# Router products in pairs on two column groups, and router weights loaded through GpSimd's queue

## The chip, the core and the metric

One core of a Trainium2 chip runs the whole program. A core has TensorE (matrix products, PE in the profile, its weight loads as PEld), VectorE (DVE), ScalarE (ACT), GpSimd (POOL) and SyncE (SP), which share an on-chip memory of 128 partitions; products go to PSUM, here eight banks `pb[0]` to `pb[7]` of 128 x 512 float32. Transfers are issued by SP, ACT and POOL, each into a queue of its own (q1, q10 and q0 in the profile), and run on the core's 16 DMA engines. The metric is device time in microseconds (us), lower is better. Before the change the median of three runs is 1541.58 us (1539.56 to 1543.03).

## The reference, cut to what matters

One decoder layer for 256 prompt tokens and 8 sample tokens, D = 2048, all in float32:

```
h  = RMSNorm(x);  q, k, v, u = h @ w_in          # 4 MB of w_in per 512 columns
x += [dilated attention | causal pooling] @ w_out
x += cross_attention(RMSNorm(x), 256 memory rows) @ w_co
h  = RMSNorm(x)
lg = h @ w_rg + b_rg                              # 4 expert groups: top 1
le = h @ w_re + b_re                              # 32 experts in 4 groups of 8: top 2 in the group
x += sum over the chosen experts of gate * SwiGLU_expert(h)
```

The step also returns the key and value caches of 8 sample rows shifted by one position: some 100 MB that are copied from DRAM to DRAM. The change concerns `lg` and `le`, which the kernel computes as one product with 36 columns.

## The kernel before, in words

Each engine runs its own written-out list of instructions, and semaphores order them; no planner is involved. All 264 tokens stand transposed in `xT`: 16 tiles of 128 channels x 264 tokens.

**Start.** SP loads the memory rows, `w_ck` in four parts, the tokens and `w_cv` (L437 to L445). ACT issues small loads first (L1279 to L1287), the last of them the router weights `w_rg` and `w_re` into `wr` (128 partitions x 16 x 36, a run of 4 or of 32 floats at a time: 2048 runs each) and the bias `b_re`. Only then does ACT square the memory rows and the tokens for the norms (L1288 to L1298). DVE makes diagonal matrices of the roots (L1635), and PE turns them into a row of scales (L705), for which it waits. Before that, PE computes the memory keys (L689) and two bias tables (L697, L699); after it the memory values and the turned tokens (L713, L718).

**Weights in a ring of two.** The 4 MB pieces (`w_ck`, `w_cv`, seven of `w_in`, `pool_w`, four of `w_out`, `w_cq`, `w_co`) go to two places in turn: `big(i)` on SP first waits until PE has used piece i - 2. PE works on them in order: L713 and L663 for `w_cv`, L663 and L669 for `w_in`, L745 for the rest of it, L909 for `w_out`, L927 for `w_cq`, L1041 for `w_co`.

**Cache copies.** ACT issues the 64 copies of the caches, 1.5 MB each, between its other work (`cache_part`, L1261), so their times follow PE's.

**GpSimd** only issues loads: constants at the start, the bias table (L596, then L599, four loads), and from L602 on the cache rows for the sample tokens, for which it waits until the sample queries are stored.

**Cross-attention's output and the router.** `for o in range(KT)` (L1037) computes the 16 channel tiles of the output: four products (L1041), DVE adds the tile to `xT` (L1872), ACT squares it, DVE adds the squares up (L1788). `route(k)` (L1014) multiplies tile k by `wr`, two tiles behind, and adds in bank 4. At the end ACT copies the 36 x 264 sums to `LT` (L1514), PE turns them to tokens (L1059), and DVE chooses experts from L1905 on. At every fourth tile the sample rows are turned (L1034).

**Experts.** SP streams the weights of 32 experts, 12.6 MB each, into the same ring and a third place; `gate_up(0, 0, 1)` (L521) waits for `w_co` to be used, the quarters of expert 1 (L495) for the first products of expert 0 (L1157).

`router_landed` is waited for once, at L1779, by DVE, which then scales `wr` by the norm's gains (L1780); PE waits for that at L1011.

Of the kernel before, what the change touches and what calls it, by code (L numbers as in the profile page):

```python
# [15 lines left out]
P = 128  # L16
D = 2048
KT = D // P
# [3 lines left out]
TOK = SEQ + NB  # L22
# [12 lines left out]
NG, EG = 4, 8  # L35
NE = NG * EG
# [111 lines left out]
def hybrid_decoder_layer(nc, a):  # L148
    with ExitStack() as ctx:
# [3 lines left out]
        def sb(name, shape, dt=F32):  # L153
            return ctx.enter_context(nc.sbuf_tensor(name, shape, dt))
# [5 lines left out]
        xT = sb("xT", [P, KT, TOK])  # L160
# [3 lines left out]
        ident = sb("ident", [P, P])  # L164
# [16 lines left out]
        slots = sb("slots", [P, 2, 3])  # L181
        gates = sb("gates", [P, 2, 3])
        ov_i = sb("ov_i", [1, OVB + 1], I32)
        top_i = sb("top_i", [P, 3, 8], U32)
# [97 lines left out]
        xn = Z[:, 3 * D:6 * D].rearrange("p (t n) -> p t n", t=3)  # L282
        LT = wr[:].rearrange("p k n -> p (k n)")[0:36, 0:TOK]
        xfree = xT[:].rearrange("p k t -> p (k t)")
# [273 lines left out]
        def _(pool):  # L558
# [39 lines left out]
            for r in range(0, P, REPS):  # L598
                pool.dma_start(bias[r:r + REPS],  # L599
                               bass.AP(tensor=bias_dram.tensor, offset=P - 1 - r, ap=[[384 - 1, REPS], [384 * REPS, H], [1, SEQ]]))\  # L600
                    .then_inc(bias_landed, 16)
            pool.wait_ge(pads_ready, 1)  # L602
            pool.wait_ge(mem_stored, 2 * 16)
# [32 lines left out]
        def _(pe):  # L636
# [377 lines left out]
            def route(k):  # L1014
                pe.wait_ge(co_added, k + 1)
                last = mm(pb[4][0:36, 0:TOK], wr[:, k, :], xT[:, k, :], start=(k == 0), stop=(k == KT - 1))  # L1016
                if k == KT - 1:
                    last.then_inc(logits_filled, 1)
# [18 lines left out]
            for o in range(KT):  # L1037
                if o >= 4:
                    pe.wait_ge(co_added, o - 3)
                for h in range(XH):  # L1040
                    last = mm(pb[o % 4][:, 0:TOK], wo[:, h, P * o:P * o + P], oT[:, h, :], start=(h == 0), stop=(h == XH - 1))  # L1041
                last.then_inc(co_filled, 1)
                if o >= 2:
                    route(o - 2)
                if o >= 5 and o % 4 == 1:
                    sample_rows_back((o - 5) // 4)
# [10 lines left out]
            for t in range(3):  # L1057
                n = P if t < 2 else NB
                last = turn(bk[0:n, 36 * t:36 * t + 36], LT[:, P * t:P * t + n], ident[0:36, 0:36])  # L1059
            last.then_inc(v_filled, 1)  # L1060
# [173 lines left out]
        def _(act):  # L1234
# [49 lines left out]
            act.dma_start(grow[4 * KT + UT:NGAIN], a["cq_norm_g"]).then_inc(first_landed, 16)  # L1284
            for w, lo, n in (("w_rg", 0, NG), ("w_re", NG, NE)):
                act.dma_start(wr[:, :, lo:lo + n], a[w][0].rearrange("(k p) n -> p k n", p=P)).then_inc(router_landed, 16)  # L1286
            act.dma_start(b36[:, NG:36], a["b_re"].to_broadcast([P, NE])).then_inc(router_landed, 16)  # L1287
            act.wait_ge(zeros_ready, 2)  # L1288
# [224 lines left out]
            act.wait_ge(logits_filled, 1)  # L1513
            copy(LT, pb[4][0:36, 0:TOK]).then_inc(logits_copied, 1)  # L1514
            roots(st[:, 3:6], st[:, 6:9])
# [41 lines left out]
        def _(dve):  # L1557
# [14 lines left out]
            def link(ins):  # L1572
                nonlocal nseq
                nseq += 1
                ins.then_inc(dve_seq, 1)
                dve.wait_ge(dve_seq, nseq)
# [201 lines left out]

            dve.wait_ge(router_landed, 3 * 16)  # L1779
            TT(wr[:], wr[:], gT[:, 3 * KT:4 * KT].unsqueeze(2).to_broadcast([P, KT, 36]), ALU.mult).then_inc(wr_scaled, 1)  # L1780

# [341 lines left out]
```

## Time and profile before

| | |
|---|---|
| median of 3 runs | 1541.58 us |
| profiled execution | 1531.4 us, its span 1529.6 us |
| PE busy | 1269.7 us (83%) |
| DVE, ACT, POOL busy | 531.1, 167.7, 62.6 us |
| DMA | 609.34 MB, mean 398 GB/s |
| mean granted TensorE clock | 0.888 of 2.4 GHz |

The page counts an engine as busy while it computes; an instruction that issues a transfer stands under the engine's queue (ACTq, SPq). DMA share is the mean busy share of the 16 DMA engines; it can go a little over 1, since packets overlap. The chain is the sequence of work that ended last, followed back from the end; its shares sum to the span.

### The profile page before, as it was taken

The page shows a single profiled execution, that of the slowest core. Times are in us where ns is not written, and L with a number is a line of the kernel's source. Part 1 is how long each engine was busy: PE and PEld are TensorE (multiplying, and loading weights), DVE is VectorE, ACT ScalarE, POOL GpSimd, SP SyncE. Part 2 cuts the span into 40 slices and gives each one's busy share as a digit, 9 for nine tenths or more (in the row PEclk, how much of TensorE's full clock was granted, in tenths as well). Part 3 has the DMA queues.
Part 4 walks back from the last instruction along what each step waited for, and adds up shares of the span by engine and source line. Part 5 has one row for each costly group of instructions (what it writes and reads, how often), then busy time and mean ns, then how long its engine had stood idle before and what let it go on. Part 6 is the DMA issues. An engine that isn't in the chain of part 4 may idle for free.

```text
span 1529.6 us, 23145 instructions
## 1 busy us (share of the span) xinstructions
PE 1269.7 (83%) x9913; PEld 626.5 (41%) x9913; DVE 531.1 (35%) x1102; ACT 167.7 (11%) x395; POOL 62.6 (4%) x115
## 2 busy tenths in 40 slices
PE   7799999998999999887867777777787677778777
PEld 4354458774887866322222222222222222222222
DVE  1040064750112334534334333433433433333344
ACT  0410012321111244000000000000000000000000
POOL 2000012212010000000000000000000000000000
PEclk9899999999999999988888788878887878778789
DMA  9999999989999999999999999999999999999997
GB/s 346 316 332 399 327 329 382 382 311 375 379 399 400 359 389 355 403 429 426 429 433 426 430 432 431 425 429 434 425 429 434 425 429 434 425 429 429 431 428 309
DMA packets 101909, 609.34 MB, mean 398 GB/s; under 512 B 11390, under 2 KB 13065, under 8 KB 78929
## 3 DMA queue, kind: packets, MB, share of 16 engines
q1 hardware_dynamic: 55027, 477.14, 75.0%
q10 hardware_dynamic: 38822, 101.11, 18.1%
q0 software_dynamic: 8016, 30.46, 5.7%
q8 instruction: 33, 0.54, 0.1%
q14 instruction: 11, 0.09, 0.0%
HBM read 603.09 MB, written 106.75 MB: 464 GB/s over the span
## 4 chain that ended last, share of the span: by engine, by line
DMA 53%; PE 40%; ACTq 3%; DVE 1%; issue 1%; ACT 1%; SPq 1%; DVEq 0%
DMA ring<-in_w_e_up_dram 44%; PE pb L1157 12%; PE pb L663 6%; PE pb L909 6%; DMA ring<-in_w_out_dram 5%; DMA ring<-in_w_in_dram 4%; PE pb L745 4%; ACTq L1286 2%; PE pb L1041 2%; PE pb L927 2%; PE pb L713 1%; SPq L486 1%; PE pb L669 1%; PE pb L1016 1%; PE pb L1191 1%
## 5 line engine op out<-in xcount | busy, mean ns | idle before, releaser
L1157 PE MATMUL pb<-ring,xT 128*32 128x256 f32 x4096 | 285.7, 441 | 123.4 <-DMA ring<-in_w_e_up_dram 118.7
L1157 PEld LDWEIGHTS pb<-ring,xT 128*32 128x32 f32 x4096 | 143.5, 126 | 285.7 <-DMA ring<-in_w_e_up_dram 156.5
L2040 DVE TENSOR_TENSOR Z<-pb,Z 128x512 f32<-128x512 f32 x248 | 152.7, 679 | 253.1 <-PE pb L1110 253.1
L1093 PE MATMUL pb<-Z,xT 128*32 128x512 f32 (+1 forms) x768 | 137.1, 808 | 94.8 <-DVE Z L2040 91.7
L1110 PE MATMUL pb<-xT 32*128 32x512 f32 x744 | 168.7, 751 | 0.0
L1191 PE MATMUL pb<-ring,xT 128*32 128x512 f32 x960 | 136.9, 722 | 0.0
L663 PE MATMUL pb<-ring,hreg 128*128 128x512 f32 (+1 forms) x320 | 125.7, 552 | 2.6 <-DMA ring<-in_w_in_dram 2.6
L1093 PEld LDWEIGHTS pb<-Z,xT 128*32 128x32 f32 (+1 forms) x768 | 16.6, 117 | 185.7 <-DVE Z L2040 118.9
L663 PEld LDWEIGHTS pb<-ring,hreg 128*128 128x128 f32 x320 | 60.1, 190 | 65.1 <-issue 59.2
L909 PE MATMUL pb<-hreg,ring 128*128 128x264 f32 x320 | 78.3, 402 | 5.8 <-DMA ring<-in_w_out_dram 5.8
L745 PE MATMUL pb<-hreg,ring 128*128 128x264 f32 x320 | 75.3, 395 | 1.0 <-DMA ring<-in_w_in_dram 1.0
L2037 DVE TENSOR_TENSOR Z<-pb,Z 128x512 f32<-128x512 f32 x31 | 21.4, 692 | 144.7 <-remote 84.1
L909 PEld LDWEIGHTS pb<-hreg,ring 128*128 128x128 f32 x320 | 62.3, 199 | 17.0 <-DMA ring<-in_w_out_dram 6.5
L745 PEld LDWEIGHTS pb<-hreg,ring 128*128 128x128 f32 x320 | 61.2, 194 | 13.4 <-DMA ring<-in_w_in_dram 1.4
L1191 PEld LDWEIGHTS pb<-ring,xT 128*32 128x32 f32 x960 | 32.1, 130 | 78.2 <-issue 77.5
L2064 DVE TENSOR_SCALAR xT<-xT 128x128 f32<-128x128 f32 x32 | 7.3, 227 | 148.4 <-ACT xT L1533 148.4
L1110 PEld LDWEIGHTS pb<-xT 32*128 32x128 f32 x744 | 30.5, 154 | 67.0 <-issue 67.0
L1533 ACT ACTIVATE xT<-pb 128x128 f32<-128x128 f32 x32 | 8.9, 278 | 421.8 <-PE pb L1157 421.8
L1535 ACT COPY xT<-pb 128x264 f32<-128x264 f32 x32 | 12.2, 381 | 313.9 <-PE pb L1102 313.9
L1791 DVE TENSOR_TENSOR xT<-pb,xT 128x264 f32<-128x264 f32 x16 | 6.9, 433 | 111.6 <-PE pb L909 111.6
L909 PE MATMUL pb<-Z,ring 128*128 128x264 f32 x192 | 45.4, 386 | 0.0
L1657 DVE COPY Z<-pb 128x512 f32<-128x512 f32 (+1 forms) x5 | 3.2, 638 | 104.5 <-PE pb L663 104.5
(333 smaller groups left out, 1117.2 us busy)
## 6 DMA issues: line engine op xcount, KB each, us to landing
ring<-in_w_e_gate_dram SPq DMA_DIRECT2D x61, 2048.0 KB, 18.6
ring<-in_w_e_up_dram SPq DMA_DIRECT2D x61, 2048.0 KB, 23.1
ring<-in_w_e_down_dram SPq DMA_DIRECT2D x30, 4096.0 KB, 18.9
out_win_k_sample_dram<-in_cache_win_k_dram ACTq DMA_DIRECT2D x24, 1536.0 KB, 15.4
out_win_v_sample_dram<-in_cache_win_v_dram ACTq DMA_DIRECT2D x24, 1536.0 KB, 14.0
ring<-in_w_in_dram SPq DMA_DIRECT2D x7, 4096.0 KB, 32.9
ring<-in_w_out_dram SPq DMA_DIRECT2D x4, 4096.0 KB, 32.7
out_win_k_sample_dram<-in_cache_win_k_dram ACTq DMA_DIRECT2D x8, 1488.0 KB, 15.0
```

The costliest lines, as they stand in the source:

```text
L663: last = mm(bk[:, 0:n], xt[:, k, tile * P:tile * P + P], w[:, k, 0:n], start=(k == 0), stop=(k == KT - 1))
L745: last = mm(bk[:, 0:TOK], w[:, k, :], hT[:, k, :], start=(k == 0), stop=(k == KT - 1))
L909: last = mm(bk[:, 0:TOK], w[:, k, :], mix(k), start=(i == 0), stop=(i == KT - 1))
L927: last = mm(bk[:, 0:TOK], wk(CQ)[:, k, XD * h:XD * h + XD], xT[:, k, :], start=(k == 0), stop=(k == KT - 1))
L1041: last = mm(pb[o % 4][:, 0:TOK], wo[:, h, P * o:P * o + P], oT[:, h, :], start=(h == 0), stop=(h == XH - 1))
L1093: last = mm(pb[0][32 * c:32 * c + 32, :], pick[0:n, t, :], xn[0:n, t, 512 * c:512 * c + 512], start=(t == 0), stop=(t == 2))
L1110: last = mm(out, GT[r, cols], yo[r, :], start=True, stop=True)
L1157: last = mm(pb[1][32 * c:32 * c + 32, 0:256], XT[:, k, :], w[:, :, k8, P * c:P * c + P], start=(k == 0), stop=(k == KT - 1))
L1191: last = mm(pb[3][32 * c:32 * c + 32, :], aT[:, 32 * f:32 * f + 32], w[f][:, 512 * c:512 * c + 512], start=(f == 0), stop=(f == 3))
L1286: act.dma_start(wr[:, :, lo:lo + n], a[w][0].rearrange("(k p) n -> p k n", p=P)).then_inc(router_landed, 16)
L2037: last = V.tensor_tensor(x3s, banks[0][:, :], x3s, ALU.add)
L2040: last = V.tensor_tensor(d, banks[c][:, :], d, ALU.add)
```

## The change

Two things are changed. The three loads of the router's weights and of `b_re` go from ACT's list, ahead of its squares, to GpSimd's list, behind the four loads of the bias table. And `route` is called in pairs after every odd tile: even tiles go to partitions 0 to 35 of bank 4, odd tiles to partitions 64 to 99 (another group of TensorE's columns), each half with its own start and stop; the two halves are copied by two ACT instructions, and the turn to tokens becomes a product with `both36`, two identities stacked at rows 0 and 64 with zeros between, so that it adds the halves. Of `LT` the rows 36 to 63 hold what is left of `wr`, and meet zeros.

```
+        both36 = sb("both36", [P, 36])
-        LT = wr[:].rearrange("p k n -> p (k n)")[0:36, 0:TOK]
+        LT = wr[:].rearrange("p k n -> p (k n)")[:, 0:TOK]
 GpSimd, behind the bias table's loads:
+            for w, lo, n in (("w_rg", 0, NG), ("w_re", NG, NE)):
+                pool.dma_start(wr[:, :, lo:lo + n], a[w][0].rearrange("(k p) n -> p k n", p=P)).then_inc(router_landed, 16)
+            pool.dma_start(b36[:, NG:36], a["b_re"].to_broadcast([P, NE])).then_inc(router_landed, 16)
             pool.wait_ge(pads_ready, 1)
 TensorE:
             def route(k):
                 pe.wait_ge(co_added, k + 1)
-                last = mm(pb[4][0:36, 0:TOK], wr[:, k, :], xT[:, k, :], start=(k == 0), stop=(k == KT - 1))
+                r = 64 * (k % 2)
+                last = mm(pb[4][r:r + 36, 0:TOK], wr[:, k, :], xT[:, k, :], start=(k < 2), stop=(k >= KT - 2))
...
-                if o >= 2:
+                if o >= 3 and o % 2:
+                    route(o - 3)
                     route(o - 2)
...
-                last = turn(bk[0:n, 36 * t:36 * t + 36], LT[:, P * t:P * t + n], ident[0:36, 0:36])
+                last = mm(bk[0:n, 36 * t:36 * t + 36], LT[0:100, P * t:P * t + n], both36[0:100, :], start=True, stop=True)
 ScalarE, start:
-            for w, lo, n in (("w_rg", 0, NG), ("w_re", NG, NE)):
-                act.dma_start(wr[:, :, lo:lo + n], a[w][0].rearrange("(k p) n -> p k n", p=P)).then_inc(router_landed, 16)
-            act.dma_start(b36[:, NG:36], a["b_re"].to_broadcast([P, NE])).then_inc(router_landed, 16)
 ScalarE, behind the loop:
-            copy(LT, pb[4][0:36, 0:TOK]).then_inc(logits_copied, 1)
+            copy(LT[0:36], pb[4][0:36, 0:TOK])
+            copy(LT[64:100], pb[4][64:100, 0:TOK]).then_inc(logits_copied, 1)
 VectorE, behind its wait for router_landed:
+            link(V.memset(both36[:], 0.0))
+            V.tensor_copy(both36[0:36], ident[0:36, 0:36])
+            V.tensor_copy(both36[64:100], ident[64:100, 64:100])
```

## Rows read from the trace of the kernel before

**Rows 1.** The page's chain that ended last, shares of the span by line.

```profile
DMA ring<-in_w_e_up_dram 44%; PE pb L1157 12%; PE pb L663 6%; PE pb L909 6%; DMA ring<-in_w_out_dram 5%; DMA ring<-in_w_in_dram 4%; PE pb L745 4%; ACTq L1286 2%; PE pb L1041 2%; PE pb L927 2%; PE pb L713 1%; SPq L486 1%; PE pb L669 1%; PE pb L1016 1%; PE pb L1191 1%
```

**Rows 2.** The chain in order of time, 0 to 60 us: start, us, what.

```profile
5.57 30.33 ACTq L1286
35.94 3.18 ACTq L1287
...
54.76 2.00 PE pb L713 x2
...
57.16 1.06 PE pb L713 x2
```

**Rows 3.** The timeline, 0 to 60 us: start, us, engine, line; brackets: idle before, releaser.

```profile
20.82 0.30 PEld L689 LDWEIGHTS pb<-ring 128*128 128x128 f32 x2 [1.30 <-DMA ring<-in_w_ck_dram]
...
42.36 0.80 PE L699 MATMUL pb<-qkm,psm 33*128 33x321 f32 x2
...
53.02 1.74 PE L705 MATMUL pb<-Z,ones 128*128 128x128 f32 x6 [9.86 <-DVE Z L1635]
```

**Rows 4.** Stretches at the start and of a w_in piece: last columns PEclk, DMA share, GB/s.

```profile
37.50:42.50 5.00, 5.00 (x13) 1.76 (x12) 0.00 (x0) 3.28 (x4) 0.00 (x0) 1.00 0.65 59
80.00:93.00 13.00, 13.00 (x36) 6.01 (x35) 11.55 (x28) 1.05 (x4) 0.00 (x0) 1.00 0.70 229
93.00:125.80 32.80, 31.99 (x197) 15.81 (x196) 3.69 (x4) 2.69 (x7) 0.00 (x0) 1.00 1.03 387
```

**Rows 5.** The one DMA issue of 92.5 to 93.2 us: size, us to landing.

```profile
ring<-in_w_in_dram SPq DMA_DIRECT2D x1, 4096.0 KB, 32.9
```

**Rows 6.** TensorE's timeline, 120 to 178 us, where it starts on the second and third piece.

```profile
125.48 14.00 PE L663 MATMUL pb<-ring,hreg 128*128 128x512 f32 x32 [0.81 <-DMA ring<-in_w_in_dram]
158.78 14.00 PE L663 MATMUL pb<-ring,hreg 128*128 128x512 f32 x32 [1.76 <-DMA ring<-in_w_in_dram]
```

**Rows 7.** DMA packets and queues of 5 to 42 us, then of 700 to 1400 us.

```profile
DMA packets 6342, 12.42 MB, mean 336 GB/s; under 512 B 5034, under 2 KB 5203, under 8 KB 5305
q10 hardware_dynamic: 4612, 0.37, 11.2%
DMA packets 17186, 300.72 MB, mean 430 GB/s; under 512 B 1904, under 2 KB 1904, under 8 KB 1904
```

**Rows 8.** POOL's timeline: the bias table's loads and the next one.

```profile
64.48 2.48 POOL L599 DMA_DIRECT2D ring<-bias_rows  x4 [9.41 <-DMA bias_rows<-qkm]
206.44 0.59 POOL L562 DMA_DIRECT2D ring<-in_cache_win_k_dram  x1 [139.49 <-DMA out_win_k_sample_dram<-Z]
```

**Rows 9.** The chain in order of time, the output loop and two comparisons: start, us, what.

```profile
292.58 0.80 PE pb L792 x8
...
561.39 0.57 PE pb L1016 x2
561.96 1.98 PE pb L1041 x8
...
570.12 1.78 PE pb L1041 x8
...
614.75 3.63 PE pb L1157 x64
```

**Rows 10.** DVE's timeline, 366 to 376 us.

```profile
370.61 0.74 DVE L1780 TENSOR_TENSOR wr<-wr,gT 128x576 f32<-128x576 f32 x1
```

**Rows 11.** The timeline behind the loop, 590 to 600 us.

```profile
596.91 0.63 PEld L1053 LDWEIGHTS pb<-ones,Z 128*128 128x128 f32 x6 [0.48 <-DVE Z L1788]
596.95 0.37 ACT L1514 COPY wr<-pb 36x264 f32<-36x264 f32 x1 [0.56 <-PE pb L1016]
597.57 0.34 PE L1059 MATMUL pb<-ident,wr 36*128 36x36 f32 x3
```

**Rows 12.** Stretches behind the output loop; columns as in rows 4.

```profile
588.00:598.00 10.00, 9.97 (x49) 6.33 (x48) 3.39 (x11) 3.24 (x8) 0.00 (x0) 1.00 0.88 299
612.00:616.00 4.00, 4.00 (x75) 2.27 (x67) 2.90 (x16) 0.00 (x0) 0.00 (x0) 1.00 0.65 219
```

## The prediction

> **What bounds the kernel now.** I read the page's chain first, then the chain and the timeline of its two places that the change touches, then the DMA's stretches between them. By line the chain is the stream of expert weights for nearly half of the span and products for most of the rest; a single entry is neither, ACT's queue at L1286 with 2% [rows 1]. In order of time that entry is one instruction: the issue of `w_re` holds ACT's list from 5.57 us for 30.33 us, and `b_re` for 3.18 us more [rows 2]. The squares behind it give the scales late: PE has ended its last bias table (L699) at 43.16 us and stands still for 9.86 us, until L705 at 53.02 us [rows 3]. So the start is bound by an issue, not by data.
>
> From 93 us on the DMA is full, share 1.03 [rows 4]: a 4 MB piece of `w_in` issued there needs 32.9 us to land [rows 5], and PE waits for the pieces, 0.81 and 1.76 us at the second and third [rows 6]. At the output loop the chain is PE's products alone [rows 9]; at its end and behind it the DMA has a little room, 0.88 for 10 us and 0.65 for 4 us [rows 12]. Behind it the experts' stream runs at 430 GB/s [rows 7] to the end; it can only be moved earlier as a whole.
>
> **The change part by part.** All against the profiled execution, 1531.4 us.
>
> *ACT without the issues.* 33.5 us of issues go [rows 2]. ACT then squares as soon as rows and tokens are there, and what is late next is PE itself, which cannot take the scales before it has ended L699. So not 33.5 us are won but PE's idle time, 9.86 us. Beside it goes the clock's price: after the pause L705 takes 1.74 us [rows 3] and the first pair of L713 2.00 us, where a later pair takes 1.06 [rows 2]. The engine had stood still, and half speed (1.2 of 2.4 GHz) doubles an instruction; L705 at half its time wins 0.87, L713 0.94, together 1.8 us. Third, the small packets of `w_rg` and `w_re` leave the first loads alone: the weight loads' 1.30 us of waiting for `w_ck` [rows 3] may shrink; the bounds are 0 and 1.3, I take 1.0. PE reaches the memory values 9.9 + 1.8 + 1.0 = 12.7 us earlier.
>
> *The same loads on GpSimd.* POOL has two waits that could be touched: the four loads of the bias table stand ahead, so they lose nothing; behind, POOL waits 139.49 us for the sample queries until 206.44 us [rows 8], or to 194 us when all is 12.7 us earlier. How long POOL needs to issue runs of 16 and 128 bytes, no row shows. Bounds: 0.62 us each, as L599's four in 2.48 us [rows 8], and ACT's 33.5 us in all [rows 2]. I take the first for the sum; either is hidden by that wait: from about 56 us (the bias loads' end, 67 us, less 11) the cover lasts 138 us. The data is wanted at 370 us, where DVE scales it [rows 10].
>
> *The DMA's share.* The packets do not go away. Between 5 and 42 us ACT's queue took 11.2% of 16 engines, 4.1 us of all of them; from the other side, 336 GB/s moved there against 430 GB/s later [rows 7] leaves 37 x (1 - 336/430) = 8.1 us. That work now lies behind 56 us, where room is scarce: 37.5 to 42.5 us had 0.35 x 5 = 1.8 us free and 80 to 93 us 0.30 x 13 = 3.9 us [rows 4], and both close, since ACT's copies stand behind its squares and now begin earlier. The cost on the path is what the second and third piece of `w_in` land later than 12.7 us ahead of now. In the full stretch SP's queue gets its part whatever the backlog of the copies, and a piece takes 32.9 us either way [rows 5]; a third queue slows it only while the small packets last. Bounds 0 and 8.1 us; I take 2, nearest to half of the 4.1, since some of it falls before the piece is issued. That the copies' own backlog costs nothing is assumed: it is the first rival. Start, net: 12.7 - 2 = 10.7 us.
>
> *The pairs.* A `route` costs the chain 0.57 us [rows 9] and a slower restart: the eight products of a tile take 1.98 us behind it, 1.78 us behind a turn [rows 9]. So 0.57 + 0.20 = 0.77 us each. Two halves of the array at work together are shown by L792: eight matmuls in two groups of 64 columns, 4 x 256 and 4 x 128 columns long, take 0.80 us [rows 9]; one after the other at L663's rate (14.00 us for 32 of 512 columns [rows 6], 0.85 ns a column) it would be 1.31. Four groups gain more, 64 of 256 columns in 3.63 us [rows 9] against 14.0. So I price a pair at 0.77 + 0.1 us, not at 1.54: seven pairs in the loop save 7 x 0.67 = 4.7 us. Bounds: 7 x 0.20 = 1.4 us if they do not overlap at all and only a restart is saved, 7 x 0.77 = 5.4 us if the second is free.
>
> What is late next is the DMA. The copies and loads of the loop are the same, in less time. The room was 0.12 x 10 + 0.35 x 4 = 2.6 us [rows 12]; beyond that the experts' stream begins behind the same work. The share is no hard wall (1.03 in [rows 4]), so I take 3.0 us, bounds 0 and 4.7.
>
> *The end of the router.* The second ACT copy costs at most another 0.37 us, and the product with `both36` has two passes where the turn had one: 0.34 us more at most [rows 11]. The copy is hidden: PE's next work, L1053, waits for DVE's squares and not for the products [rows 11], and the last pair ends before the three products of now did. Without that cover it is 0.37 us. I count 0. DVE's three new small instructions stand ahead of the scaling at 370 us; each is far smaller than its 0.74 us [rows 10], and the loop that wants it begins 190 us later [rows 9]: 0, and 2.2 us if that cover were gone.
>
> The Trainium skill, TensorEngine Tiling, Key Properties, says that a change of the tiling mode drains TensorE. The 0.20 us restart agrees; by that rule alone, without overlap, the loop would save the lower bound.
>
> Sum: 10.7 + 3.0 = 13.7 us, so 1517.7 us for a profiled execution. That one lay 10.2 us under the median of the runs; I carry the difference over: 1541.58 - 13.7 = 1528 us. With everything kept it is 9.9 + 1.8 + 1.3 + 4.7 = 17.7 us less, 1524; with 8.1 us given back and no gain in the loop 4.6 us less, 1537.
>
> **The rivals.**
>
> *The DMA takes most of it back.* If the stretch from 93 us on is bound by the sum of its packets and not by SP's part of them, the pieces land only as much earlier as DMA room is found: 1.8 + 3.9 us [rows 4] less the 2 to 4 us of small packets, so 2 to 4 us, and 1 to 2 us at the loop. That gives 4 to 6 us, 1536 us. For it: share 1.03 and two waits of PE for pieces. Against it: 80 to 93 us had room, and two of the copies go out before PE's products for the keys end. The Trainium skill has this as a rule in DMA: Bandwidth & Descriptors, Issuing engines are not separate DMA queues: loads from another engine share the same 16 engines, and only issue time is saved. The rows bear out both halves: issue time is what the chain shows.
>
> *The pairs do not overlap.* Then the loop saves 1.4 us or nothing, the start stays: some 11 us, 1531 us. Against it are L792 and L1157 in [rows 9].
>
> *GpSimd is held as ACT was, and longer: slower than before.* If the two loads of short runs hold POOL's list, the cache rows of the sample tokens come late, and through DVE's sample scores and PE's turns the whole kernel does. It decides from the point where POOL is not free by 194 us, that is when three issues from about 56 us take over 138 us, four times ACT's 33.5 [rows 2], with now two other queues beside them. At five times, 167 us, everything behind is 30 us late, less 13.7: 16 us slower, 1558 us. Against it: L599's 0.62 us an issue [rows 8].
>
> *It does not do what it says.* Some other condition holds the scales back, such as the tokens' landing; then the start gains under 3 us and the whole stays within the measurement's reach: 1540 us. Against it: nothing else stands ahead of ACT's squares but landings, and PE's keys and tables last to 43 us [rows 3].
>
> **How the numbers follow.** Forecast (1523 to 1533) 0.60; DMA takes it back 0.19; no overlap 0.08; does nothing 0.07; slower 0.06. The likeliest gives 1528 us. The range 1522 to 1537 holds the first three but for the upper part of the second, 0.8 in all. About 0.2%, 3 us, is what a measurement of this kernel can tell from no change: faster 0.60 + 0.08 + 0.18 = 0.86, the same 0.08, slower 0.06.
>
> **What would show it.** ACT's first square at about 8 us and not behind 39 us; L705 with under 1 us of idle time ahead of it, near 42 us, at the full granted clock; the third piece of `w_in` landing near 148 us, not 158.7 (if near 155, the first rival is right). Two `route` rows beside each other in 0.6 to 0.7 us, the loop 4.7 us shorter from L1041's first to its last product; the first quarter of expert 1 issued 15 us earlier if both parts carry, with no DMA room left before it. POOL's issues of `wr` over before 100 us. An idle POOL row of less than 50 us ahead of L562 would speak for the slower case. A `w_in` wait of PE over 5 us at L663 would prove my 2 us too small.

## The result, and the profile after

The changed kernel takes 1521.1 us in the median of four runs (1518.74 to 1529.45) against 1541.47 us of the kernel before (1539.56 to 1543.03): a ratio of 0.9887, with a 95% interval of 0.986 to 0.9915, that is 17.4 us less (13.1 to 21.6). The forecast was 13.7 us less, 1528, with a range from 1522 to 1537. The direction was right and the gain was 4 us larger. The median of 1521.1 lies 0.9 us below the range; by the ratio, on the earlier median of 1541.58, the time is 1524, inside it.

The profiled execution of after took 1520.75 us, close to its median; that of before, 1531.4, lay 10 us under its own. So the two traces differ by 10.7 us where the runs differ by 17.4 (by the ratio) to 20.4 (by the medians), and a trace can show where the gain arises but not all of its size. Starts on TensorE in the two traces, with the line of before / after:

| point | before | after | shift |
|---|---|---|---|
| scales, L705 / L709 | 53.02 | 43.60 | -9.4 |
| third piece of `w_in`, L663 / L667 | 158.78 | 145.82 | -13.0 |
| output loop, L1041 / L1046 | 555.81 | 544.95 | -10.9 |
| behind the loop, L1053 / L1059 | 596.91 | 580.74 | -16.2 |
| expert 0, L1157 / L1163 | 610.75 | 594.93 | -15.8 |
| expert 1, first half of its gate and up weights | 628.28 | 613.93 | -14.4 |
| expert 1, last quarter of them | 636.29 | 623.41 | -12.9 |

The page's chain by line, against [rows 1]: ACT's queue is gone, the streams stand as before.

```profile
DMA ring<-in_w_e_up_dram 45%; PE pb L1163 12%; PE pb L667 6%; PE pb L913 5%; DMA ring<-in_w_in_dram 4%; PE pb L749 4%; DMA ring<-in_w_out_dram 2%; PE pb L931 2%; PE pb L1046 2%; PE pb L693 2%; PE pb L717 1%; PE pb L867 1%; DMA qkm<-Z 1%; SPq L487 1%; PE pb L673 1%
```

ACT's timeline of after (start, us, engine, line; in brackets the idle time before it and its releaser), against [rows 2]: the first square starts at 7.29 us, the tokens' squares wait for the tokens' landing alone, and the first copy of the caches goes out at 33.12 us.

```profile
7.29 1.91 ACT L1273 ACTIVATE hreg<-Z 128x2048 f32<-128x2048 f32 x1
...
25.81 1.91 ACT L1273 ACTIVATE hreg<-Z 128x2048 f32<-128x2048 f32 x1 [9.89 <-DMA Z<-in_x_prompt_dram]
...
33.12 0.70 ACTq L1267 DMA_DIRECT2D out_win_k_sample_dram<-in_cache_win_k_dram  x1
```

TensorE's timeline of after, against [rows 3, 6]: no pause ahead of L709, its six products in 1.03 us and not 1.74, a first pair of L717 in 1.13 us (2.08 in before), and of the first three w_in pieces only the third is waited for.

```profile
42.86 0.80 PE L703 MATMUL pb<-qkm,psm 33*128 33x321 f32 x2
43.60 1.03 PE L709 MATMUL pb<-Z,ones 128*128 128x128 f32 x6
44.55 1.13 PE L717 MATMUL pb<-ring 128*128 128x512 f32 x2
...
145.82 14.00 PE L667 MATMUL pb<-ring,hreg 128*128 128x512 f32 x32 [0.98 <-DMA ring<-in_w_in_dram]
```

POOL's timeline of after, against [rows 8]: the three issues that held ACT for 33.9 us (0.41 for `w_rg`, and the 30.33 and 3.18 of [rows 2]) take 1.18, 1.16 and 0.56 us here, and the wait behind them is still 134.87 us long.

```profile
54.95 2.48 POOL L600 DMA_DIRECT2D ring<-bias_rows  x4 [10.36 <-DMA bias_rows<-qkm]
57.41 1.18 POOL L604 DMA_DIRECT2D wr<-in_w_rg_dram  x1
58.59 1.16 POOL L604 DMA_DIRECT2D wr<-in_w_re_dram  x1
59.73 0.56 POOL L605 DMA_DIRECT2D b<-in_b_re_dram  x1
195.16 0.55 POOL L563 DMA_DIRECT2D ring<-in_cache_win_k_dram  x1 [134.87 <-DMA out_win_k_sample_dram<-Z]
```

The DMA of after, packets of 5 to 42 us:

```profile
DMA packets 2651, 13.90 MB, mean 376 GB/s; under 512 B 775, under 2 KB 938, under 8 KB 1609
```

The same of 57 to 76 us, in which the three loads are issued and land (issue lines: size, us to landing):

```profile
DMA packets 2487, 6.74 MB, mean 355 GB/s; under 512 B 165, under 2 KB 213, under 8 KB 2485
...
wr<-in_w_re_dram POOLq DMA_DIRECT2D x1, 256.0 KB, 14.7
wr<-in_w_rg_dram POOLq DMA_DIRECT2D x1, 32.0 KB, 13.9
b<-in_b_re_dram POOLq DMA_DIRECT2D x1, 16.0 KB, 14.9
```

The reader is to see two things. Of the 5034 packets under 512 B of [rows 7], 4259 have left the first 42 us. And they have not come back: between 57 and 76 us there are 165 such packets in all, while 304 KB of router weights and bias land; up to 600 us they are 4457 against 8636 in before. ACT's queue moved them in runs of 16 and 128 bytes; through GpSimd's queue the records show no such runs.

The stretches of [rows 4] in after (last columns: granted TensorE clock, DMA share, GB/s): the two holes of before, 59 and 229 GB/s, are filled.

```profile
37.50:42.50 5.00, 5.00 (x13) 1.81 (x11) 0.27 (x1) 0.00 (x0) 0.00 (x0) 1.00 0.98 360
80.00:93.00 13.00, 13.00 (x38) 6.25 (x37) 4.86 (x6) 1.07 (x2) 0.00 (x0) 1.00 1.00 365
93.00:125.80 32.80, 32.80 (x197) 16.09 (x196) 0.69 (x1) 1.62 (x5) 0.00 (x0) 1.00 1.03 397
```

Together (360 - 59) x 5 + (365 - 229) x 13 + (397 - 387) x 32.8 us make 3.6 MB more in these stretches; over the whole of 0 to 125.8 us it is 365 against 337 GB/s, 3.5 MB.

The loop in the chain of after (start, us, what), against [rows 9]: a pair of routes takes the 0.57 us that one took, and the slow restart comes once for two tiles (3.76 us for 16 products, 3.56 behind a turn).

```profile
544.95 7.36 PE pb L1046 x32
552.31 0.57 PE pb L1021 x4
552.88 3.76 PE pb L1046 x16
556.64 0.57 PE pb L1021 x4
557.21 0.53 PE pb L1039 x4
557.74 3.56 PE pb L1046 x16
...
602.95 20.42 DMA ring<-in_w_e_up_dram
```

From the loop's first product to L1053 / L1059 before took 41.10 us, after 35.79: 5.3 us less. The last row is what the texts below call the wait for expert 1 (the expectations also say: for its first quarter, but it is the last): the time from the last issue of its gate and up weights to the landing, 17.48 us in the chain of before. TensorE works during most of it; it stands still for 1.45 us ahead of that quarter's products in before and for 2.91 us in after. From L1053 / L1059 to expert 0 before takes 13.84 us and after 14.19, so the router's end costs 0.35 us.

### The profile page after: what moved, and what is told of

It reads as the page before. It is cut to its first block, busy times and chain, and to the rows that moved or that the text cites. A ratio compares the mean times of both kernels' runs of the same rounds, so it can differ in the third digit from the quotient of the medians.

```text
span 1518.9 us, 23155 instructions
## 1 busy us (share of the span) xinstructions
PE 1271.1 (84%) x9916; PEld 627.2 (41%) x9916; DVE 532.2 (35%) x1105; ACT 168.0 (11%) x396; POOL 65.5 (4%) x118
## 4 chain that ended last, share of the span: by engine, by line
DMA 54%; PE 43%; DVE 1%; SPq 1%; issue 1%; ACT 0%; POOL 0%; ACTq 0%; DVEq 0%
DMA ring<-in_w_e_up_dram 45%; PE pb L1163 12%; PE pb L667 6%; PE pb L913 5%; DMA ring<-in_w_in_dram 4%; PE pb L749 4%; DMA ring<-in_w_out_dram 2%; PE pb L931 2%; PE pb L1046 2%; PE pb L693 2%; PE pb L717 1%; PE pb L867 1%; DMA qkm<-Z 1%; SPq L487 1%; PE pb L673 1%
## 5 line engine op out<-in xcount | busy, mean ns | idle before, releaser
L1163 PE MATMUL pb<-ring,xT 128*32 128x256 f32 x4096 | 286.0, 441 | 124.2 <-DMA ring<-in_w_e_up_dram 121.2
L1163 PEld LDWEIGHTS pb<-ring,xT 128*32 128x32 f32 x4096 | 142.9, 126 | 288.2 <-DMA ring<-in_w_e_up_dram 161.8
L1197 PE MATMUL pb<-ring,xT 128*32 128x512 f32 x960 | 142.3, 746 | 0.0
L667 PE MATMUL pb<-ring,hreg 128*128 128x512 f32 (+1 forms) x320 | 125.4, 552 | 1.0 <-DMA ring<-in_w_in_dram 1.0
L667 PEld LDWEIGHTS pb<-ring,hreg 128*128 128x128 f32 x320 | 60.2, 190 | 63.2 <-issue 59.5
L913 PE MATMUL pb<-hreg,ring 128*128 128x264 f32 x320 | 76.1, 394 | 3.6 <-DMA ring<-in_w_out_dram 3.6
L749 PE MATMUL pb<-hreg,ring 128*128 128x264 f32 x320 | 73.6, 388 | 1.7 <-DMA ring<-in_w_in_dram 1.7
L913 PEld LDWEIGHTS pb<-hreg,ring 128*128 128x128 f32 x320 | 60.6, 194 | 14.4 <-DMA ring<-in_w_out_dram 4.1
## 6 DMA issues: line engine op xcount, KB each, us to landing
ring<-in_w_in_dram SPq DMA_DIRECT2D x7, 4096.0 KB, 32.2
```

What stands on the lines that cost most here:

```text
L667: last = mm(bk[:, 0:n], xt[:, k, tile * P:tile * P + P], w[:, k, 0:n], start=(k == 0), stop=(k == KT - 1))
L749: last = mm(bk[:, 0:TOK], w[:, k, :], hT[:, k, :], start=(k == 0), stop=(k == KT - 1))
L913: last = mm(bk[:, 0:TOK], w[:, k, :], mix(k), start=(i == 0), stop=(i == KT - 1))
L1163: last = mm(pb[1][32 * c:32 * c + 32, 0:256], XT[:, k, :], w[:, :, k8, P * c:P * c + P], start=(k == 0), stop=(k == KT - 1))
L1197: last = mm(pb[3][32 * c:32 * c + 32, :], aT[:, 32 * f:32 * f + 32], w[f][:, 512 * c:512 * c + 512], start=(f == 0), stop=(f == 3))
```

## The experiments

Ratios are to the kernel before, run on the same chip.

**1. The loads alone.**

```
 before, with:
-            act.dma_start(wr ...), act.dma_start(b36 ...)
+            pool.dma_start(wr ...), pool.dma_start(b36 ...)   # behind the bias loads
```

> The kernel before with one part of the change: w_rg, w_re and b_re go through GpSimd's queue, behind the bias loads; the routes stay single. Theory A (the start is bound by ACT's held queue, the loop by TensorE): TensorE reaches the output loop about 11 us earlier than in the kernel before (544 to 546 us against 555.8), the loop keeps its 41 us from L1041 to L1053, and expert 1's first quarter lands about 10 us earlier, since the DMA's little room behind the loop is not touched; 9 to 12 us faster as a whole. Rival B (the DMA is full from 40 to 600 us, and what is begun earlier is given back in its queue): the landing of expert 1's first quarter moves by under 6 us.

Measured: 1526.65 us, ratio 0.9881 (0.9846 to 0.9916), 18.4 us less. The pause is gone, and the loop is as long as before (551.25 to 592.36, 41.1 us). TensorE's timeline of this kernel:

```profile
42.75 0.80 PE L702 MATMUL pb<-qkm,psm 33*128 33x321 f32 x2
43.48 1.02 PE L708 MATMUL pb<-Z,ones 128*128 128x128 f32 x6
```

So within the intervals the loads alone give as much as the whole change, and more than theory A's 9 to 12 us: it had the place right and the size too small. The profiled execution, 1533.72 us, was the slowest of its six (TensorE waits 6.20 us for a piece of w_in at 250 us); still its loop begins 11.2 us ahead of experiment 2's on the same chip, whose start is that of before. Rival B is out.

**2. The pairs alone.**

```
 after, with:
-            pool.dma_start(wr ...), pool.dma_start(b36 ...)
+            act.dma_start(wr ...), act.dma_start(b36 ...)     # where they stood before
```

> The kernel before with the other part: routes in pairs on two column groups and the stacked identity; the loads stay on ACT. Theory A: the start is unchanged (TensorE idle for 9 to 10 us ahead of L705), the loop is 5.3 us shorter on TensorE, but TensorE then waits longer for expert 1's first quarter (20 us against 17.5), so that 2 to 3 us are left at the end. Rival B (no room in the DMA at all): under 1 us faster. Rival C (TensorE sets the time behind the loop): all 5 us arrive.

Measured: 1540.11 us, ratio 0.9969 (0.9942 to 0.9996): 4.8 us less (0.6 to 9.0). All three expectations but the smallest lie in that. The loop is 5.3 us shorter, as said (562.41 to 598.21). What was not expected stands at the start, where this kernel equals the one before. TensorE's timeline:

```profile
53.01 1.75 PE L706 MATMUL pb<-Z,ones 128*128 128x128 f32 x6 [10.01 <-DVE Z L1639]
54.69 2.08 PE L714 MATMUL pb<-ring 128*128 128x512 f32 x2
```

The granted clock behind it (last columns clock, DMA share, GB/s):

```profile
54.00:58.00 4.00, 4.00 (x10) 2.13 (x9) 1.00 (x4) 0.38 (x1) 0.70 (x1) 0.50 1.03 365
58.00:62.00 4.00, 4.00 (x8) 1.54 (x7) 0.00 (x0) 0.38 (x1) 0.00 (x0) 0.50 1.02 343
62.00:66.00 4.00, 4.00 (x14) 1.88 (x12) 0.00 (x0) 0.76 (x2) 1.62 (x3) 0.76 0.76 241
```

The same two stretches in the trace of before:

```profile
54.00:58.00 4.00, 4.00 (x11) 2.00 (x10) 1.00 (x4) 0.38 (x1) 0.70 (x1) 0.67 1.05 381
58.00:62.00 4.00, 4.00 (x16) 2.09 (x15) 0.00 (x0) 1.14 (x3) 0.00 (x0) 1.00 1.04 346
```

Behind the same pause the clock stays at half speed for 11 us in one trace (0.76 of the last four) and for under 4 in the other. The memory values took 26.8 us here, 23.5 in before and 22.6 in after. The third piece of w_in started at 164.68 us and not at 158.78. The trace that the prediction was read from was thus a mild case of the pause.

**3. Pairs in one column group.** The loads on GpSimd, and the routes two at a time into one accumulation of 36 partitions (against experiment 1):

```
-                if o >= 2:
+                if o >= 3 and o % 2:
+                    route(o - 3)
                     route(o - 2)
```

> The first experiment, and the routes called two at a time as in the changed kernel, but both into the same 36 partitions of one accumulation, with the single copy and the turn of before. It tells what the pairing saves without a second column group. If the gain of the loop is overlap of two halves of the array, only a restart of 0.2 us per pair is saved: the loop is 1 to 1.6 us shorter than in the first experiment, and a pair takes 1.1 us in the chain. If pairing in order alone does it, the loop is 4 to 5.5 us shorter and a pair takes under 0.8 us. At the end 0.5 to 1.6 us faster than the first experiment by the first view.

Measured: 1525.38 us, ratio 0.9877 (0.9844 to 0.991). The loop takes 38.8 us: 2.3 less than with single routes, 3.0 more than with two groups. In the chain of this kernel a pair takes 1.01 us:

```profile
552.62 1.01 PE pb L1019 x4
553.63 3.76 PE pb L1044 x16
```

So the first view, that the gain is overlap, was right in kind; it had put what the pairing saves without overlap too low (1 to 1.6 us). Beside the one restart of 0.20 us a second route in the same group costs 0.44 us and not 0.57, together 0.33 a pair. In the second column group the second route costs nothing, another 0.44 us a pair: the overlap is full.

**4. The loads first.** The changed kernel with the three loads at the head of GpSimd's list:

```
+            pool.dma_start(wr ...), pool.dma_start(b36 ...)
             for dst, src in ((rb[0:NBUCKET], a["rel_bias"]), ...
...
-            pool.dma_start(wr ...), pool.dma_start(b36 ...)   # behind the bias loads
```

> The changed kernel with the three router loads at the head of GpSimd's list, so that their small packets move in the first 40 us as in the kernel before, while ACT's queue stays free. If the time on ACT's queue is all of the start's cost (theory A), ACT's first square stays at 7 to 8 us, TensorE's idle time ahead of L709 stays under 1 us and the loop begins within 1 us of the changed kernel's 544.95. If the packets themselves cost 1 to 4 us in the first loads (rival D), TensorE waits 1 to 4 us more for w_ck or for the tokens before 45 us, and the loop begins later by as much, less what the freer DMA behind 57 us gives back (at most 2 us).

Measured: 1526.51 us, ratio 0.9882 (0.9848 to 0.9916). The loop begins at 550.35 us, 5.4 later than in the changed kernel; L709 has no pause but starts at 47.20 and not 43.60 us. Rival D's size came true, by another way. TensorE's timeline of this kernel, then of the changed one:

```profile
12.07 2.82 PE L683 MATMUL pb<-ident,Z 128*128 128x128 f32 x16 [2.26 <-DVE ring L1625]
15.47 0.39 PE L686 MATMUL pb<-ident,Z 75*128 75x75 f32 x1 [0.58 <-DMA Z<-in_cq_norm_g_dram]
15.65 8.69 PE L693 MATMUL pb<-ring 128*128 128x512 f32 x14
```

```profile
10.72 3.65 PE L683 MATMUL pb<-ident,Z 128*128 128x128 f32 x16 [0.87 <-DVE ring L1625]
14.16 0.33 PE L686 MATMUL pb<-ident,Z 75*128 75x75 f32 x1
14.29 9.88 PE L693 MATMUL pb<-ring 128*128 128x512 f32 x22
```

The second set of turns and the gains of the norms come 1.4 us late, and behind these waits 14 products take 8.69 us where 22 took 9.88: the granted clock is 0.50 from 14 to 20 us, where after has 1.00, and all 64 products of L693 take 30.15 us and not 27.90. The weights of w_ck were not waited for. Two limits: through GpSimd's queue the small packets did not appear here either (814 under 512 B in 5 to 42 us, 775 in after, 5034 in before), so what they cost by themselves is not tested; and the 5.4 us at the loop are within the spread of the other kernels with the loads on GpSimd (539.9 to 551.3). By the start of the trace the place behind the bias loads is the better one; the runs do not tell the two apart (0.9882 here, 0.9887 and 0.9876 for the changed kernel). What this run does show is that the gain of 18 us stays when the loads go out at the very start again, as long as they do not stand in ACT's queue.

**5. The changed kernel again**, on the chip of the next three, unchanged.

> The changed kernel once more, to stand on the same chip as the next three. Theory A (two gains that add up, 17 us at the start with the typical kernel before and 2 to 4 us behind the loop): 0.986 to 0.989 of the kernel before. TensorE's wait for expert 1's first quarter is 19 to 21 us again.

Measured: 1522.92 us, ratio 0.9876 (0.9838 to 0.9914), and 20.5 us from the last issue for expert 1 to its landing, as expected.

**6 and 7. Without the copies in the loop.** The kernel before and the changed one, each without five parts of the cache copies, which stay out of the output:

```
             for o in range(KT):
                 tile_square(o, co_added, o + 1, KT - 1)
-                if o in (0, 3, 6, 9, 12):
-                    cache_part()
```

> The kernel before without the five parts of the cache copies that ACT issues in the output loop (7.7 MB read and written; that part of the caches is left out of the output). It has no other DMA to wait for behind the loop than the experts' weights. Theory A (the DMA is full behind the loop, so its bytes set when expert 1 begins): TensorE's wait for expert 1's first quarter falls from 17.5 us to 5 us or less, 12 to 17 us faster than the kernel before. Rival (the quarter's landing is set by when its issue is released, not by what else moves): the wait stays over 14 us.

> The changed kernel without the same five parts of the copies. Theory A: with the DMA no longer full behind the loop, the whole 5.3 us of the pairs pass on: this one lies 4.5 to 5.5 us more below the previous kernel at the end than the start's shift alone explains (2 to 3 us in the pair with copies), and the wait for expert 1's first quarter is within 1.5 us of that kernel's. Rival (half of the pairs' gain is lost to something other than the DMA, such as the router's longer end): the difference stays at 2 to 3 us.

Measured: 1541.88 us, ratio 0.9999 (0.9977 to 1.002), and 1524.37 us, ratio 0.9877 (0.9843 to 0.9912). Taking 7.7 MB away won nothing that these intervals show (3.5 us either way for the first, 5 for the second), and the two differ by 17.5 us where before and experiment 5 differ by 20.6: no sign that more of the pairs arrives without the copies, though a difference of 2 us would not be seen. Theory A, that the DMA's bytes behind the loop hold expert 1 up by 12 to 17 us, falls. It had taken the 17.5 us for TensorE's idle time, which was 1.45. A stretch of experiment 6 (clock, DMA share, GB/s):

```profile
572.00:596.00 24.00, 24.00 (x102) 15.20 (x102) 7.26 (x19) 6.51 (x14) 0.00 (x0) 1.00 0.01 2
```

Its first issue on SP behind the loop:

```profile
595.08 0.33 SPq L486 DMA_DIRECT2D ring<-in_w_e_gate_dram  x1
```

And the wait for expert 1 in its chain:

```profile
618.35 18.78 DMA ring<-in_w_e_up_dram
```

The DMA now stands still for 24 us, and still expert 0's second half is issued only at 595.08 us, when the loop's last product is over, since it goes into the ring half that the loop reads. It is the same in before (595.49) and in after (579.33, with the last product over at 579.31). The wait for expert 1 is 18.8 us long here, where the DMA had stood idle before, and was 17.48 in before, where it had been full; in experiment 7 it is 17.9 (20.4 and 20.5 in after and experiment 5). The experts' stream begins when the loop's last product is over, so a shorter loop begins it earlier.

**8. Copies in the gaps.** The changed kernel with three of the five parts moved to stretches where its trace shows an idle DMA:

```
+                        if not done: cache_part()            # behind the first key norm
-                    cache_part(2 if j == 7 else 1)
+                    cache_part(2 if j in (7, 9) else 1)
             cross_exps(0)
-            cache_part()
+            cache_part(2)
-                if o in (0, 3, 6, 9, 12):
+                if o in (0, 6):
```

> The changed kernel with three of the five parts of the copies moved out of the output loop into stretches where the trace of the changed kernel shows an idle DMA: one behind the first of the key norms (idle at 190 to 198 us), one at the tenth channel (318 to 323 us), one at the first cross scores (524 to 530 us). Nothing is left out. Theory A (behind the loop the DMA's bytes are the bound): the wait for expert 1's first quarter falls from 20 us by 6 to 10 us, and the kernel is 5 to 9 us faster than the changed one. Rival (the gaps are filled at the cost of loads that TensorE waits for soon after): the loop begins 3 us or more later and under 3 us are won.

Measured: 1521.59 us, ratio 0.9875 (0.9843 to 0.9908), 1.3 us under experiment 5, which the runs cannot tell from nothing. The wait for expert 1 is 18.84 us long: 1.6 less, not 6 to 10. The loop began at 544.19 us, so the rival's price was not paid either; there was just little to win, as 6 and 7 say.

**9. The pause filled.** The kernel before with products ahead of L705:

```
-            pe.wait_ge(diag_ready, 1)
             bk = vbank("scale")
+            for _ in range(36):
+                mm(bk[:, 0:P], ident[:], ident[:], start=True, stop=True)
+            pe.wait_ge(diag_ready, 1)
```

> The kernel before, with 36 products of the identity by itself (results not used) on TensorE in its pause ahead of L705; nothing else is changed, and ACT's queue is held as before. Theory C (what the start costs beyond the pause of 9.9 us is the granted clock, which falls to 0.50 behind the pause and comes back at a time that differs from run to run, 56 to 63 us): the clock stays 1.00, L705 takes 1.0 us and not 1.74, the memory values (L713) 22.6 us and not 23.5 to 26.8, the first w_in product starts at 76 to 77 us; 2 to 5 us faster than the kernel before, so that the change's 17 to 20 us split into some 10 of pause, 2 to 5 of clock and the rest. Rival (the extra of the start is the DMA's, whose copies begin late): the clock is as said, but TensorE waits as much longer for the second and third piece of w_in, and under 1 us is won.

Measured: 1539.32 us, ratio 1.0005 (0.9981 to 1.0029). TensorE's timeline:

```profile
43.45 8.30 PE L703 MATMUL pb<-ident 128*128 128x128 f32 x72
54.19 1.03 PE L707 MATMUL pb<-Z,ones 128*128 128x128 f32 x6 [2.43 <-DVE Z L1637]
55.15 1.74 PE L715 MATMUL pb<-ring 128*128 128x512 f32 x2
...
79.60 14.00 PE L663 MATMUL pb<-ring 128*128 128x512 f32 x32
```

The same product in before:

```profile
78.52 14.00 PE L663 MATMUL pb<-ring 128*128 128x512 f32 x32
```

The clock behind L707:

```profile
54.00:58.00 4.00, 3.81 (x12) 2.25 (x13) 2.09 (x6) 0.38 (x1) 0.70 (x1) 0.69 0.98 329
58.00:62.00 4.00, 4.00 (x13) 1.67 (x12) 0.00 (x0) 0.76 (x2) 0.00 (x0) 0.88 1.04 368
```

L707 runs at full speed, but the clock fell a little later all the same, for some 3 us, and the scales came 1.2 us later than in before. So L663 started 1.1 us later than in before, not 2 us earlier (the expectation takes it for the first w_in product; by the order of the pieces it is still w_cv, and the first w_in product follows, 1.1 us later too): in this trace the run did not do what it was made for. Nothing was won that could have gone into waiting (the third piece started at 158.39 us, 158.78 in before), and neither theory C nor its rival is tested; what the clock behind the pause costs at the end stays open.

**10 and 11. Expert 0 with the clock kept.** Experiment 1 and the changed kernel, each with

```
+                if first:
+                    for _ in range(11):
+                        mm(pb[5][:, 0:P], ident[:], ident[:], start=True, stop=True)
                 if not last_of_all:
                     gather(i + 1)
```

> The first experiment (loads on GpSimd, single routes) with 11 more products of the identity (results not used) ahead of expert 0's gather for expert 1, where TensorE stands still for 3.1 us and the granted clock has then fallen to 0.50 in five of nine traces, for 3 to 11 us. It is the partner of the next run, for the gain of the pairs with that chance taken out. Clock 1.00 from expert 0's first product to expert 1's first, which starts 17.5 us behind it. Theory C: 0 to 2 us faster than the first experiment; rival (the products come in the way of the gather): up to 1 us slower.

> The changed kernel with the same 11 products. Theory A (of the pairs' 5.3 us, 2 to 4 reach the end): 2 to 4 us faster than the previous run. Rival 1 (all of it reaches the end once the clock stays up): 4.5 to 5.5 us faster than the previous run. Rival 2 (the experts' stream takes it all): within 1 us of it. Against the changed kernel itself 1 to 4 us faster by theory C, since expert 1's first products then start 17.5 us behind expert 0's and not 19 to 22.

Measured: 1521.57 us, ratio 0.9885 (0.985 to 0.992), and 1521.43 us, ratio 0.9871 (0.9837 to 0.9905). Expert 0's gather for expert 1 on TensorE behind its pause of 3.1 us, in before, where the clock was kept, and in after, where it was lost:

```profile
621.45 2.92 PE L1093 MATMUL pb<-Z,xT 128*32 128x512 f32 x24 [3.12 <-DVE xT L2016]
```

```profile
605.64 4.39 PE L1099 MATMUL pb<-Z,xT 128*32 128x512 f32 x24 [3.12 <-DVE xT L2023]
```

The granted clock in after, and in experiment 10, same stage:

```profile
604.00:608.00 4.00, 2.36 (x12) 0.60 (x16) 3.57 (x10) 0.00 (x0) 0.00 (x0) 0.66 1.02 430
```

```profile
597.00:609.00 12.00, 11.54 (x147) 6.48 (x143) 9.52 (x33) 0.33 (x2) 0.00 (x0) 1.00 0.90 337
609.00:613.00 4.00, 4.00 (x48) 1.35 (x44) 0.87 (x2) 0.78 (x2) 0.00 (x0) 1.00 1.02 424
```

(The expectation's count was off: in the ten traces there were, the clock had fallen in six.) The fall is not spread evenly: behind this pause the clock was lost in six of the seven traces with paired routes and an unfilled pause (after and experiments 2, 3, 4, 5 and 7, not 8), and in none of the four with single routes (before and experiments 1, 6 and 9). No run shows why. The local aim was met: from expert 0's to expert 1's first product it is 17.5 us in 10, 11 and 12, where it was 19.0 in the changed kernel, 20.7 in experiment 5 and 22.4 in experiment 7. At the end little came of it: 11 is 1.5 us under 5, which is within their scatter. And the pairs are worth 0.1 us between the medians of 10 and 11, 2 us by their ratios, with an interval of 5 us to either side of each: rival 2 is favoured, theory A's 2 us are not excluded, and rival 1's 5 us are unlikely but not ruled out.

**12. Both.** Experiment 11 with the copies of 8.

> The previous run with three parts of the copies moved to the idle stretches of the DMA, as in the eighth experiment. If the backlog of copies behind the loop costs expert 1's second quarter 1.6 us, as the wait of 18.8 us against 20.4 says, it is 1 to 2 us faster than the previous run; if that wait is chance, within 1 us of it.

Measured: 1518.16 us, ratio 0.9856 (0.9821 to 0.9892), the fastest of all, 3.3 us under experiment 11 by the medians; six runs of each overlap (1513.29 to 1522.1 against 1517.36 to 1522.92), so that the gain is likely and not shown.

## Why the prediction was right, and where it was not

The mechanism of the start was right and its size too small; the mechanism of the pairs on TensorE was right, and how much of it reaches the end is open. That the sum of 13.7 us came within 4 us of the measured 17.4 is partly luck: the loads alone give 18 us where the sum had 10.7, and the pairs on top of them 0 to 2 us where it had 3.0.

*The pause at L705 (9.86 us).* Right: it is gone in every kernel with the loads on GpSimd, and there in all four traces with them on ACT (9.86, 10.01 and 10.65 us; filled by other work in experiment 9). What was late next was TensorE itself, as said. Up to the first w_in product the shift is 11.1 us (93.23 to 82.12), where the sum had 12.7.

*The clock (1.8 us).* Right in the two traces: L709 wins 0.7 to 0.8 and the first pair of L717 0.95. The size is one of a mild case: in experiment 2 the memory values alone took 4.3 us longer than in after, in before only about 1. What of it reaches the end is not shown: experiment 9 gains nothing (2.9 us less to 4.5 us more), but there the clock fell behind L707.

*The wait for w_ck (1.0 us).* Failed: the wait fell from 1.30 to 0.28 us, but TensorE had begun the keys 1 us later (14.29 and 13.26 us) and ended L703 0.5 us later than before.

*The issue on GpSimd.* Right: 2.9 us in all against bounds of 1.9 and 33.5, hidden by the long wait. The case "slower" had asked for 138 us.

*The DMA's share (-2 us).* This step failed, in sign. It had the small packets come back behind 56 us. They do not (165 under 512 B in 57 to 76 us). Something that the sum had put at nothing may work for the change: the first parts of the copies go out 19 us earlier (33.12 and 51.92 us), into the first hole of [rows 4], and the second closes with the next w_in issue, 11 us earlier. So 3.5 MB more have moved by 125.8 us, and the third piece of w_in is ready 13.0 us earlier, more than the 11.1 us of TensorE's shift and of the piece's issue: it landed 32.2 us behind its issue, in before 34.0. That the earlier copies did this is read from the two traces and not shown: no experiment moved the copies' begin alone, and the same landing took 32.6 us in experiment 9, with late copies, and 33.9 in experiment 1, with early ones. The forecast was 148 us, its rival's 155; it is 145.8. Over all traces the third piece starts at 158.4 to 164.7 us with the loads on ACT (four) and at 145.3 to 147.4 with them on GpSimd behind the bias loads (nine): 14.8 us between the means, where the sum had 10.7 net. At the output loop the means of the same traces are only 11.9 us apart (555.4 to 562.4 against 539.9 to 551.3 us).

The Trainium skill, DMA: Bandwidth & Descriptors, Issuing engines are not separate DMA queues, says that issuing on several engines saves only the sequencer's time, usually small beside the transfer. The trace differs in the second half: ACT's issue of `w_re` took 30.33 us [rows 2] and landed its 256 KB in 35.4, GpSimd's issue 1.16 and the landing 14.7.

*The pairs (4.7 us on TensorE, 3.0 net).* On TensorE 5.3 us, at the upper bound of 5.4: I had given the second route 0.1 us, and it costs none (experiment 3 tells the 3.0 us of overlap from the 2.3 that going in pairs saves by itself). Six pairs, not seven, stand between the loop's products; the seventh saving is a route that now runs behind the loop, while TensorE waits for DVE anyway. The net is what the runs cannot settle: 4.8 us (0.6 to 9.0) alone, 0 to 2 on top of the loads. The reason given for the loss, a full DMA, is not confirmed: the stream is released by the loop's last product, and without the copies nothing more arrived (experiments 6 and 7). In the traces the copies do cost something near the 1.7 us that the prediction took off: the wait for expert 1 is 19.8 to 20.5 us in the changed kernel with all of them (after, experiments 4, 5 and 11) and 17.9 to 18.8 with three or five parts moved or left out (7, 8 and 12). A second loss, which the prediction did not have, is the clock lost in expert 0, 1.5 to 4.9 us, in six of seven traces with paired routes and no filler. Neither is seen further on: from the loop's last product to expert 2's first it is 56.2 to 63.1 us over all traces, whichever kernel, a scatter larger than the pairs' gain.

*The end of the router (0).* 0.35 us: the three products with both36 take 0.73 us in the chain of after, the turns took 0.28 in experiment 1, and that is on the path; the copies' 0.37 us is not.

*The rivals.* "The DMA takes most of it back" and "does nothing" fall with the third piece at 145.8 us and ACT's square at 7.29; "no overlap" falls with the pair of 0.57 us; "slower" falls with POOL's issues of 2.9 us.

What stays open: by the runs the loads alone win 18 us (experiments 1 and 10), by the traces 14.8 at the third piece and 11.9 at the loop. The profiled runs of the kernels with the loads on ACT lay 10, 1.4, 7.6 and 0.2 us under the medians of their kernels, 4.8 on average, where the nine traces with the loads on GpSimd behind the bias loads lay on average at theirs; so the traces may be mild cases, which would account for most of the gap. No trace shows where the missing 3 to 6 us arise.

## What to carry to other kernels

A load of many short runs is to be judged by the queue that issues it: look for an issue of tens of microseconds at the head of an engine's list, and move it to an engine that is about to wait anyway. When such a queue comes free, ask what else stood behind it; here copies began 19 us earlier, into stretches where the DMA had moved only 59 and 229 GB/s, which may have helped the next stage. And before a full DMA is blamed for a lost gain, look at what releases the next issue, and at whether the engine stands still while it waits: here the release was TensorE's own last product, it stood still for 1.45 us of the 17.5, and taking away 7.7 MB changed nothing that the runs can see.

## What the runs showed of the hardware that was not expected

- The same loads cost 33.9 us of issue on ACT's queue and 2.9 us on GpSimd's, and 4179 packets under 512 B (of 8636 up to 600 us) vanished from the records.
- Two products of 36 columns on two column groups took 0.57 us, as long as one; in one group 1.01.
- Behind a pause of 10 us the granted clock stayed at 0.50 for under 4 us in one trace and 11 in another; behind one of 3.1 us ahead of expert 0's gather it fell in six of eleven traces, all six with paired routes, and in none of three where products filled the pause.
